# Two gated linear attentions in a fused transformer block: state chunks of 32 tokens instead of 16, with inner blocks of 4 and products at three levels

## What is computed

```python
def gla_chunked(q, k, v, log_a, scale):        # c = LA_BLOCK = 16 in the reference
    ...
    G = jnp.cumsum(log_a..., axis=3)           # within a chunk, per key channel
    rel = G[r] - G[s] for s <= r, else -inf
    a_intra = einsum('rd,sd,rsd->rs', q, k, exp(rel))
    o_intra = a_intra @ v
    q_in = q * exp(G);  k_out = k * exp(G_last - G);  a_chunk = exp(G_last)
    # over chunks:  o_inter = q_in @ state
    #               state = state * a_chunk + k_out^T @ v
    return o_intra + o_inter
```

## Time and profile before

| | us |
|---|---|
| median of 3 executions | 1896.93 (1896.34 to 1897.4) |
| the profiled execution, its own time | 1896.46 |
| its span, first to last instruction | 1894.6 |
| PE busy | 1846.2 (97%) |
| DVE busy | 932.2 (49%) |
| ACT busy | 728.5 (38%) |
| POOL busy | 211.2 (11%) |
| mean granted TensorE clock | 0.986 of full |

### The profile page before, as it was taken

The page is one execution under the profiler, slowest core; times in us unless marked ns, Lnnn a source line. Parts: engine busy times, 40 slices in busy tenths (PEclk is TensorE's granted clock), DMA queues, the critical chain, the costliest instruction groups (busy, mean ns, idle before and its releaser), DMA issues.

```text
span 1894.6 us, 27514 instructions
## 1 busy us (share of the span) xinstructions
PE 1846.2 (97%) x10095; PEld 1495.0 (79%) x10095; DVE 932.2 (49%) x1309; ACT 728.5 (38%) x1067; POOL 211.2 (11%) x180
## 2 busy tenths in 40 slices
PE   8999899899999999999999999999999999999998
PEld 6787567587888888888888888888776778888887
DVE  6453576646776743345544334333667353443322
ACT  6535533545444432322342323233555342332222
POOL 0030001021111110000111111101000211111110
PEclk9999987999999999999999999999999999999999
DMA  6302100123333333333333333333330233333331
GB/s 188 89 25 57 45 24 23 67 78 89 100 89 99 97 92 101 99 94 95 100 93 96 100 96 92 92 101 97 85 92 1 66 90 100 90 98 97 92 98 69
DMA packets 309228, 160.97 MB, mean 85 GB/s; under 512 B 12688, under 2 KB 306832, under 8 KB 309024
## 3 DMA queue, kind: packets, MB, share of 16 engines
q1 hardware_dynamic: 308080, 157.21, 28.7%
q0 software_dynamic: 640, 2.17, 0.3%
q10 hardware_dynamic: 432, 0.52, 0.1%
HBM read 157.79 MB, written 2.10 MB: 84 GB/s over the span
## 4 chain that ended last, share of the span: by engine, by line
PE 93%; DVE 3%; ACT 2%; issue 1%; DMA 1%; POOL 0%; ACTq 0%; DVEq 0%; POOLq 0%
PE ps L372 27%; PE ps L373 27%; PE ps L374 27%; PE ps L1726 1%; PE ps L1474 1%; PE ps L1484 1%; PE ps L1181 1%; PE ps L1092 1%; PE ps L2022 1%; PE ps L2023 1%; PE ps L922 1%; PE ps L1717 1%; DVE xlo L446 0%; ACT whi L359 0%; DMA mx<-in_x 0%
## 5 line engine op out<-in xcount | busy, mean ns | idle before, releaser
L372 PE MATMUL ps<-xhi,whi 128*128 128x512 f32 x1656 | 657.4, 397 | 3.4 <-DVE wlo L367 2.3
L373 PE MATMUL ps<-xlo,whi 128*128 128x512 f32 x1656 | 647.6, 391 | 0.0
L374 PE MATMUL ps<-xhi,wlo 128*128 128x512 f32 x1656 | 647.6, 391 | 0.0
L359 ACT ACTIVATE whi<-raw 128x1024 fp32r<-128x1024 f32 (+2 forms) x297 | 309.0, 1040 | 707.5 <-PE ps L374 706.9
L367 DVE TENSOR_TENSOR wlo<-raw,whi 128x1024 fp32r<-128x1024 f32 (+2 forms) x297 | 365.0, 1229 | 280.4 <-ACT whi L359 280.4
L372 PEld LDWEIGHTS ps<-xhi,whi 128*128 128x128 f32 x1656 | 312.9, 189 | 72.7 <-issue 4.8
L373 PEld LDWEIGHTS ps<-xlo,whi 128*128 128x128 f32 x1656 | 312.9, 189 | 66.3 <-issue 2.6
L374 PEld LDWEIGHTS ps<-xhi,wlo 128*128 128x128 f32 x1656 | 312.7, 189 | 65.7
L622 DVE TENSOR_TENSOR zS<-ps,rs 128x512 f32<-128x512 f32 x132 | 91.3, 692 | 296.7 <-PE ps L374 284.5
L374 PE MATMUL ps<-h_hi,wlo 128*128 128x512 f32 x528 | 205.4, 389 | 0.0
L372 PE MATMUL ps<-h_hi,whi 128*128 128x512 f32 x528 | 205.4, 389 | 0.0
(11 more groups left out here) (334 smaller groups left out, 1559.3 us busy)
## 6 DMA issues: line engine op xcount, KB each, us to landing
raw<-in_conv_ffn_w SPq DMA_DIRECT2D x52, 512.0 KB, 3.8
raw<-in_mla_ffn_w SPq DMA_DIRECT2D x52, 512.0 KB, 3.8
raw<-in_w_up SPq DMA_DIRECT2D x44, 512.0 KB, 3.8
raw<-in_w_in SPq DMA_DIRECT2D x28, 512.0 KB, 3.9
raw<-in_conv_w_in SPq DMA_DIRECT2D x24, 512.0 KB, 3.7
raw<-in_w_down SPq DMA_DIRECT2D x16, 448.0 KB, 3.7
raw<-in_conv_ffn_w SPq DMA_DIRECT2D x16, 448.0 KB, 3.6
raw<-in_mla_ffn_w SPq DMA_DIRECT2D x16, 448.0 KB, 3.7
```

Of the source, the lines that this page charges most:

```text
L359: a.activation(whi[:, u % PARTS, 0:n], raw[:, u % RAW, 0:n], ACT.Copy).then_inc(hi_split, 1)
L372: t_.matmul(out, wh, xh, start=first, stop=False)
L373: t_.matmul(out, wh, xl, start=False, stop=False)
L374: return t_.matmul(out, wl, xh, start=False, stop=last)
```

## The change

It makes a chunk 32 tokens with inner blocks of 4. Pairs in the same block of 4 are summed stepwise as before, with distances 0 to 3 (128 * (4 - j) columns each). Pairs in different blocks of the same chunk are made by products at three levels, with halves of 4, 8 and 16 tokens: at each level all keys by the queries of the second halves (`near(b)`), masked to the same pair of halves (`mask(b)`). The keys and queries are lengthened between the levels, in place, by the products of the neighbouring blocks (`longer(b)`), so that after the third level they are k_out and q_in. The values by the masked products of all three levels and the products with the states are all summed by PE in one bank per value tile, which DVE adds once. The masked tiles of the level of 16 are 128 columns wide; their first halves are zeroed once by POOL.

The matmuls of each attention, before and after (counts from the program):

| | gla before | gla after | hg (each) before | hg (each) after |
|---|---|---|---|---|
| near, 64 columns | 16 | 3 x 16 | 8 | 3 x 8 |
| far | 16 of 64 columns | 16 of 128, 32 of 64 | 8 of 64 | 8 of 128, 16 of 64 |
| intra, columns | 2 x 2304 | 2 x 1280, on 64 rows each | 2304 | 1280 |
| chunk states | 64 of 128 columns | 64 of 64 | 32 of 128 | 32 of 64 |
| inter | 124 of 16 columns | 60 of 32 | 62 of 16 | 30 of 32 |
| fills, k steps | 16 | 16 | 16 | 16 |

The core of the diff:

```diff
-LC = 16
+LC = 32
 NL = T // LC
-HC = LC // 2
+HC = 4
+NEAR_BLOCKS = (4, 8, 16)
...
+            def near(b):
+                outs = [pe_ring(pe, f"{nm} near{b} {h}") for h in range(n_heads)]
+                pe.wait_ge(*after(f"{nm} q{b}"))
+                for t in range(TT):
+                    blk = slice(t * P, (t + 1) * P)
+                    for h in range(n_heads):
+                        rows = slice(L["dk"] * h, L["dk"] * (h + 1))
+                        last = t_.matmul(outs[h][:, t * DH:(t + 1) * DH].rearrange("p (n c) -> p n c", c=b),
+                                         keys[rows, blk], which_half(queries[rows, blk], 1, b), start=True, stop=True)
...
+            def intra(j):
+                n = T // HC * (HC - j)
...
+                if nm == "gla":
+                    for vi, rows in enumerate(HEAD_ROWS):
+                        t_.matmul(outs[vi], C(f"gla{vi}")[rows, :], prod[rows], start=True,
+                                  stop=True).then_inc(*step("pe", f"gla intra{j} {vi} full"))
...
             def far_values():
-                for vi in range(len(L["v"])):
-                    out = pe_ring(pe, f"{nm} far{vi}")
...
+                for vi, out in enumerate(outs):
+                    for t in range(TT):
+                        tile = out[:, t * P:(t + 1) * P]
+                        for b in (16, 8, 4):
+                            dst = tile if b == 16 else which_half(tile, 1, b)
+                            n = P if b == 16 else DH
+                            for i, rows in enumerate(HEAD_ROWS):
+                                at = t * P + DH * i
+                                t_.matmul(dst[rows], V_TOKENS[nm][vi][:, at:at + DH],
+                                          near_tile(b, 2 * vi + i)[:, t * n:(t + 1) * n],
+                                          start=t == 0 and b == 16, stop=False)
...
+            near(4)
+            fill(2)
+            intra(0)
+            near(8)
+            fill(2)
+            also(0)
+            intra(1)
+            near(16)
+            fill(2)
+            also(1)
+            pe_transpose(pe, f"{nm} ko", keys, f"{nm} q32")
+            intra(2)
+            fill(2)
+            chunk_states()
+            fill(2)
+            intra(3)
+            also(2)
+            fill(2)
+            outs = [pe_ring(pe, f"{nm} inter{vi}") for vi in range(nv)]
+            pe.wait_ge(*after(f"{nm} near16 {n_heads - 1} taken"))
+            far_values()
+            fill(4)
+            inter()
...
+            def longer(b):
+                dve.wait_ge(*after(f"{nm} near{b} {n_heads - 1} full"))
+                for name, x, second in ((f"{nm} k{2 * b}", mx[:, KO, :], 0), (f"{nm} q{2 * b}", mx[:, QI[nm], :], 1)):
+                    x = which_half(x, second, b)
+                    other = products_of(b)[:, :, 1 - second].unsqueeze(2).to_broadcast([P, T // (2 * b), b])
+                    v.tensor_tensor(x, x, other, ALU.mult).then_inc(*step("dve", name))
...
+            prod(0)
+            longer(4)
+            decay(1)
+            mask(4)
+            prod(1)
+            longer(8)
+            weigh(0)
+            mask(8)
+            also(0)
...
-            for nm in LA:
-                pool_la_setup(pool, nm)
+            pool_la_setup(pool, "gla")
+            pool_near_zeros(pool)
+            pool_la_setup(pool, "hg0")
+            pool_la_setup(pool, "hg1")
```

More of the change, by code:

```diff
@@ L1374, in pool_la_setup, with pool_near_zeros @@
                 *step("pool", f"{nm} scan inputs"))
-        def last_far(nm):
-            return f"{nm} far{len(LA[nm]['v']) - 1} full"
+        def pool_near_zeros(pool):
+            pool.wait_ge(*after("gdn o7 full"))
+            g.memset(which_half(wtile(NEAR[16], 4), 0, 16), 0.0).then_inc(*step("pool", "near zeros"))
         def act_la_decays(act, nm, ready):
@@ new lines, in pe_la, with fill @@
+            keys, queries = mx[:, KO, :], mx[:, QI[nm], :]
+            k_steps = iter(range(2 * KT))
+            def fill(n):
+                for _ in range(n):
+                    s = next(k_steps)
+                    pe_in(pe, unit + s // KT, (s % KT, s % KT + 1))
+            def near(b):
[7 more added lines that the diff above has]
+                                         keys[rows, blk], which_half(queries[rows, blk], 1, b), start=True, stop=True)
+                        if t == TT - 1:
+                            last.then_inc(*step("pe", f"{nm} near{b} {h} full"))
@@ new lines, in intra @@
+            def intra(j):
+                n = T // HC * (HC - j)
+                outs = [pe_ring(pe, f"{nm} intra{j} {vi}")[:, 0:n] for vi in range(nv)]
+                pe.wait_ge(*after(f"{nm} prod{j}"))
+                prod = PROD[j % 3][:, 0:n]
+                if nm == "gla":
+                    for vi, rows in enumerate(HEAD_ROWS):
+                        t_.matmul(outs[vi], C(f"gla{vi}")[rows, :], prod[rows], start=True,
+                                  stop=True).then_inc(*step("pe", f"gla intra{j} {vi} full"))
+                else:
+                    t_.matmul(outs[0], C("hsum"), prod, start=True, stop=True).then_inc(
+                        *step("pe", f"{nm} intra{j} 0 full"))
@@ L1438, in chunk_states @@
                             if t == TT - 1 and row + L["dk"] == P:
                                 last.then_inc(*step("pe", f"{nm} kv{r} full"))
-            pe.wait_ge(*after(f"{nm} q_near"))
-            outs = [pe_ring(pe, f"{nm} near{h}") for h in range(n_heads)]
-            for t in range(TT):
-                for h in range(n_heads):
-                    rows = slice(L["dk"] * h, L["dk"] * (h + 1))
-                    tile = pair[rows, t * P:(t + 1) * P]
-                    last = t_.matmul(outs[h][:, t * DH:(t + 1) * DH].rearrange("p (n c) -> p n c", c=HC), tile,
-                                     which_half(tile, 1), start=True, stop=True)
-                    if t == TT - 1:
-                        last.then_inc(*step("pe", f"{nm} near{h} full"))
@@ new lines, in mask @@
+            def mask(b):
+                if (nm, b) == ("gla", 16):
+                    dve.wait_ge(*after("near zeros"))
+                for h in range(n_heads):
+                    bank = full(dve, f"{nm} near{b} {h}")[:, 0:T // 2]
+                    only = C(f"near{b}")
+                    if b == 16:
+                        dst = which_half(near_tile(b, h), 1, b).rearrange("p (t n) c -> p t n c", t=TT)
+                        bank = bank.rearrange("p (t n c) -> p t n c", t=TT, c=b)
+                        only = only.rearrange("p (n c) -> p n c", c=b).unsqueeze(1).to_broadcast([P, TT, 4, b])
+                    else:
+                        dst, bank = (x.rearrange("p (t c) -> p t c", t=TT) for x in (near_tile(b, h), bank))
+                        only = only.unsqueeze(1).to_broadcast([P, TT, DH])
+                    v.tensor_tensor(dst, bank, only, ALU.mult).then_inc(*step("dve", f"{nm} near{b} {h} taken"))
@@ new lines, in dve_la @@
+            prod(0)
[7 more added lines that the diff above has]
+            also(0)
+            decay(2)
+            prod(2)
+            longer(16)
+            weigh(1)
+            mask(16)
+            decay(3)
+            prod(3)
+            add(1)
+            also(1)
+            weigh(2)
+            add(2)
+            dve.wait_ge(*after(f"{nm} chunk decays"))
+            dve.wait_ge(*after(f"{nm} kv3 taken"))
@@ L2335, in in_hg1 @@
             def in_hg1(j):
[L2336 to L2337 removed]
+                if j in (0, 2):
+                    pe_head_norm(pe, "fox qk", range(j, j + 2))
             pe_la(pe, "hg0", in_hg0, 25)
```

300 lines of the change are left out of this document (113 added, 187 removed).

## The result

The changed kernel takes 1871.72 us (median of 4 executions, 1871.32 to 1877.01) against 1896.63 for the kernel before on the same chip (4 executions): a ratio of 0.9875, interval 0.9857 to 0.9894, that is 24.9 us less. The profile is of the slowest of the four executions, 1877.01 us with a span of 1875.2.

The account below looks back on a forecast made before the run. PE, busy for 97% of the span, was taken as the bound; in the changed stage work -10.6, waits -5 and clock -5 summed to -20.6 us, from 1896.46 to a forecast of 1876 us, range 1866 to 1887.

Parts of the forecast that it names:

- Inter: PE's products with the chunk states: 15 chunks instead of 31 at a fixed price per chunk, -10.8 us over three trains.
- Intra: PE's reductions within blocks: fewer columns, and gla's two on 64 rows each overlapping, -9.3 us (-7.2 without overlap).
- Near: PE's products between block halves: two more levels per attention with unchanged shapes, at one price, +6.4 us.
- Far: PE's values by masked products: more columns, neighbouring matmuls overlapping on two column halves, +4.5 us (+3.6 to +10.7).
- Chunk states: PE's chunk state matmuls: same count, half the columns, all four quarters in flight, -2.4 us (between 0 and -4.9).
- Changes of shape: PE switching between small products and k steps: 0.1 us per change, more groups of small products, +1 us.
- Waits: PE's waits in the changed stage: 8.4 us against 13, so -5 us (-7 to -2).
- The clock: PE's half-clock spells in the changed stage: shorter trains and fewer waits before them, -5 us (between 0 and -9).
- Far without overlap: Rival: far products on two column halves run one after the other, 6.2 us more, 1882 us; chance 20%.
- A chain that is not covered in hg: Rival: four steps between levels in hg0 and hg1 each wait 2 us, +8, 1884 us; chance 7%.
- The case of 1868: Rival: short trains never drop the clock and chunk states cost what their columns say, 1868 us; chance 18%.
- No change: Rival: serial near and far work with unchanged clock and states eats the gain, leaving -2 us; chance 3%.

Follow-up runs that it names:

- 7: Kernel before with inter products of every second chunk left out (16 of 31 chunks, part of the output missing): 1883.62 us, ratio 0.9925.
- 3: Changed kernel with inter products reading 64 adjacent floats as weights (the wrong numbers) instead of spread ones: 1863.84 us, ratio 0.9822 to the kernel before.
- 9: Changed kernel with gla's reductions on all 128 rows, one after the other, instead of 64 rows each: 1871.86 us, ratio 0.9863 to the kernel before.
- 10: Kernel before with gla's reductions on 64 rows each, all else as before: 1897.01 us against 1897.6, ratio 0.9998.
- 2: Changed kernel with far products one column half of the array at a time instead of alternating: 1877.56 us, ratio 0.9897 to the kernel before.
- 8: Changed kernel with the last four k steps behind the inter products instead of ahead: 1874.22 us, ratio 0.9877 to the kernel before.
- 1: Changed kernel timed and profiled again without any edit: 1874.76 us against 1897.44 for the kernel before, ratio 0.9881.
- 4: Changed kernel with the sixteen k steps of each attention moved to where PE waits: 1868.92 us, ratio 0.9847 to the kernel before.
- 6: Kernel before with ACT copying the states side by side for the inter products, k steps not moved: 1901.52 us, ratio 1.0022.
- 5: Changed kernel with k steps moved to PE's waits and ACT copying the states side by side for inter: 1860.45 us against 1897.11 for the kernel before.

## Why the prediction was right

**The sum.** Forecast from profile to profile was -20.6; the two profiles of the change gave -19.5 and -24.0, the medians -24.9 and -22.7. It is right, with the median 1 to 4 us lower than forecast, in the range. That it comes so near is in part luck, since misses cancel: against the forecast near is up to 2.0 dearer, intra 1.5 and the chunk states 0.9 cheaper, and in the first profile 2 us more lie outside the stage than before, where the forecast had nothing. Part by part, work first:

- *Inter*, -10.8 forecast, -10.6 measured. That a chunk has a price that neither heads, columns nor clock change was read rightly from the earlier trace rows; 7 showed it by halving them. What sets it, the spread of the weights (3), the prediction did not ask, and the largest gain lay there.
- *Intra*, -9.3 forecast, -10.8 measured. gla's reductions after cost 3.1 us where 2.4 were forecast; before they cost 10.9, not the 8.1 that the column price gives, because three of the pairs ran at half clock. The 2.8 us belonged to the clock. hg's fell by 2.9 where 3.6 were forecast, one pair of them at half clock after (285.85, 1.84 us). The column price of 1.75 ns is a little high: it takes the 1.88 us of line 922's row, while the distance to the next start (223.25 to 224.97) gives 1.68. The overlap of row groups was taken rightly (9), but counted as time; 9 and 10 show that in both kernels it only exchanges work for waits.
- *Near*, +6.4 forecast, +8.4 and +7.2 measured. "This has one price" was wrong by the clock: gla's second level starts behind two waits at half clock, for 1.92 us instead of 1.05. With the stage's other near products at full clock (2, 3, 8) it is +7.0.
- *Far*, +4.5 forecast, +4.1 measured. The overlap of two column halves, for which the trace of before had only the chunk states as a hint and 20% were set against, is shown by 2: 7.67 us with it, 14.0 without. The Trainium skill, "TensorEngine Tiling (Array Packing)", Tiling Modes, gave an estimate of +3.6; the measurement agrees that the two tiles work at once, and its +4.1 lies between that and the forecast.
- *Chunk states*, -2.4 forecast, -3.3 measured: mis-sized. gla's call takes 1.48 us in place of two of 1.24 and 1.08 (the prediction took 1.24 for both), so halved columns count for more than the middle of the two bounds.
- *Changes of shape*, +1 forecast, without a row of their own in the table. A fill begins behind other work at 21 places where it was 24, and its first two matmuls are 0.31 us apart behind transposes on all 128 rows too (241.60 and 241.91 after), against 0.33 behind small products. So the 0.1 us is not shown to be the price of a change of shape, and the k steps meet it less often, not more.
- *Transposes.* A step that the prediction left out ("outside this stage nothing is changed but some constants loaded early"): k_out of gla is transposed in the stage now and was ahead of it before. It costs +0.6 inside and gives 1.3 ahead, with the wait for it (1). That is part of what the forecast was short of.

**Waits**, -5 forecast, -5.3 measured (13.03 to 7.74), and at the named places: 2.3 forecast and 2.26 found at the first reduction, 1.6 and 1.45 at the second level for the banks, 1.9 and 1.67 at the transposes behind the gdn output's norm, and in small pieces 1.5 in gla and 0.85 in hg, where 1.3 were forecast for each. Walking the order with the rows' durations was good for this. 4 shows that 4 us of them could go too.

**The clock**, -5 forecast. The k steps, whose number doesn't change, became 4.6 and 5.0 us cheaper; intra holds 2.8 more for before, near takes back 1.3. That is about -6. The reason was half right. "K steps 0.23 apart right behind the inter trains' successors" fell: behind two of three trains the clock is at half in both profiles, for 3.4 or 6.8 us in place of spells of 6.8 to 13.7 us before, and 8 finds it behind all three. What makes it fall is not shown: it fell at 13 of 18 trains of 3.4 us with spread weights and at none of six of 1.9 us with weights side by side, which differ in both length and spread, and no run tells the two apart. In 6 trains with weights side by side lie at half clock too, but they are longer (5.0 to 6.7 us) and each had a wait of 2 to 3 us ahead. The feared case, half clock through the stage, is refuted by a mean of 0.91.

**The rivals.** Far without overlap: refuted by 2. A chain that is not covered in hg: refuted by waits of 0.8 us there, none of them at a near product. The case of 1868 had its cheap chunk states half right and its clock wrong. "No change" needed the far products without overlap and falls with them. Why the median of the first comparison lies at 1871.7 and of the second at 1874.8 with the same kernel is not settled; the two profiles tie only a part of such a difference to where the half-clock spells fall.

## What to carry to other kernels

Cut the number of small matmuls with spread weights first, and ask before that whether the weights can lie side by side: that nearly halved a price which size, heads and clock did not touch. Here it paid where other work covered the copy and the clock was full (5), and lost where neither was so (6). Where PE is the bound and its clock drops, price an edit by what it does to waits and to the work behind it too: 4.7 us of work took 8.3 out of the stage (3), 6.3 us more put in 4.6 (2), and 2.2 more put in 0 to 1 (9). A saving that ends in front of a wait is not one; walk the new order with the durations of the trace to see which.

## What the runs showed of the hardware that was not expected

- A matmul with 64 columns of float32 weights that lie 64 or 128 bytes apart costs the same at both strides and at both clocks (0.224 to 0.229 us a chunk, which is two such matmuls on 64 rows or four on 32); side by side it costs 0.125 at full clock and 0.217 at half.
- ACT needs 1.89 us to copy 960 floats out of such a spread order, at 64 bytes (5), and 1.00 for as many that repeat 15 adjacent ones; 1984 at 128 bytes took 3.61 to 3.72 (6).
- Two float32 matmuls on the two column halves, all 128 rows in use, run almost wholly at the same time when they alternate: 3.76 us against 6.84 for the same products.
- One kernel's executions differ by up to 5.7 us (1871.3 to 1877.0) without any difference in the instructions. The half-clock spells lie differently in its two profiles, and one of them is worth 1.6 us; whether they account for all of it was not shown.
